# Memory keys and values of the prompt as plain float32 matmuls from unsplit weights, in four raw buffers

## The reference, cut to what matters

```python
def mem_kv(mem, lp):                      # mem: (1, 256, 1024)
    m = rmsnorm(mem, lp["mem_norm_g"])
    k = (m @ lp["w_mem_k"]).reshape(B, N_MEM, MEM_HEADS, MEM_HEAD_DIM)   # 1024 x 1024
    v = (m @ lp["w_mem_v"]).reshape(B, N_MEM, MEM_HEADS, MEM_HEAD_DIM)   # 1024 x 1024
    return k, v
```

## Time and profile before

| | us |
|---|---|
| median of 3 runs (lowest, highest) | 1037.19 (1035.57, 1038.5) |
| the profiled execution's own time | 1035.27 |
| its span, first to last instruction | 1033.5 |
| PE busy in the span | 993.0 (96%) |
| DVE, ACT, POOL busy | 514.6, 297.3, 442.5 |
| granted TensorE clock, mean | 0.994 of full |

### The profile page before, as it was taken

One profiled execution on the slowest core, in us unless ns is written; L12 is line 12 of the kernel. 1 busy time (PEld: TensorE's weight loads), 2 busy tenths in 40 slices (PEclk: granted clock), 3 DMA queues, 4 the chain that ended last, 5 costly groups with the idle time before them and its releaser, 6 DMA issues.

```text
span 1033.5 us, 19819 instructions
## 1 busy us (share of the span) xinstructions
PE 993.0 (96%) x8516; PEld 899.7 (87%) x8516; DVE 514.6 (50%) x724; ACT 297.3 (29%) x600; POOL 442.5 (43%) x282
## 2 busy tenths in 40 slices
PE   4999999889999999999999999999999999999997
PEld 4989998656777776999965799999999999999996
DVE  2889999467555555464156366431342134114413
ACT  5432375466444443121035222210120012002222
POOL 3445688500011112455420155655555555555551
PEclk9999999999899999999999999999999999999999
DMA  6422364422557772833193033223322332232222
GB/s 173 126 76 68 96 182 146 135 93 91 206 209 283 278 284 92 285 88 88 37 391 133 2 97 88 82 82 87 97 82 82 94 91 83 85 99 83 82 82 87
DMA packets 140556, 130.39 MB, mean 126 GB/s; under 512 B 13477, under 2 KB 133170, under 8 KB 136630
## 3 DMA queue, kind: packets, MB, share of 16 engines
q1 hardware_dynamic: 134888, 88.55, 28.5%
q0 software_dynamic: 2304, 37.75, 9.4%
q10 hardware_dynamic: 3278, 2.83, 0.8%
HBM read 123.53 MB, written 5.03 MB: 124 GB/s over the span
## 4 chain that ended last, share of the span: by engine, by line
PE 82%; DVE 10%; ACT 2%; issue 1%; POOL 1%; DMA 1%; SPq 1%; ACTq 1%; DVEq 0%; POOLq 0%
PE gps L558 56%; PE gps L893 5%; PE aux L907 3%; PE aux L934 3%; PE gps L1049 1%; PE aux L849 1%; PE gps L1131 1%; PE aux L913 1%; PE gps L871 1%; PE gps L969 1%; PE gps L682 1%; PE aux L1062 1%; PE aux L1083 1%; PE aux L924 1%; DVE lt L1718 1%
## 5 line engine op out<-in xcount | busy, mean ns | idle before, releaser
L487 POOL TENSOR_SCALAR whi<-wraw 128x1024 fp32r<-128x1024 f32 (+1 forms) x110 | 114.8, 1044 | 374.5 <-PE gps L558 303.3
L558 PE MATMUL gps<-act_hi,whi 128*128 128x272 f32 x912 | 265.4, 291 | 3.5 <-DVE act_lo L1636 2.8
L558 PE MATMUL gps<-act_lo,whi 128*128 128x272 f32 x912 | 264.4, 290 | 0.0
L558 PE MATMUL gps<-act_hi,wlo 128*128 128x272 f32 x912 | 263.8, 289 | 0.0
L490 POOL TENSOR_TENSOR wlo<-wraw,whi 128x1024 fp32r<-128x1024 f32 (+1 forms) x110 | 259.5, 2359 | 9.2
L558 PE MATMUL gps<-h_hi,whi 128*128 128x272 f32 x640 | 185.7, 290 | 0.0
L558 PE MATMUL gps<-h_lo,whi 128*128 128x272 f32 x640 | 185.1, 289 | 0.0
L558 PE MATMUL gps<-h_hi,wlo 128*128 128x272 f32 x640 | 184.6, 288 | 0.0
L558 PEld LDWEIGHTS gps<-act_hi,whi 128*128 128x128 f32 x912 | 172.4, 189 | 4.1 <-issue 3.1
L558 PEld LDWEIGHTS gps<-act_hi,wlo 128*128 128x128 f32 x912 | 172.4, 189 | 0.3 <-issue 0.2
L558 PEld LDWEIGHTS gps<-act_lo,whi 128*128 128x128 f32 x912 | 172.2, 189 | 0.0
(11 more groups left out here) (362 smaller groups left out, 1526.0 us busy)
## 6 DMA issues: line engine op xcount, KB each, us to landing
wraw<-in_w_up_dram SPq DMA_DIRECT2D x32, 512.0 KB, 4.0
wraw<-in_w_down_dram SPq DMA_DIRECT2D x32, 512.0 KB, 3.6
wraw<-in_w_in_dram SPq DMA_DIRECT2D x14, 512.0 KB, 4.0
kv<-in_cache_mem_k_dram SPq DMA_DIRECT2D x7, 1024.0 KB, 7.0
kv<-in_cache_mem_v_dram SPq DMA_DIRECT2D x7, 1024.0 KB, 13.2
wraw<-in_w_mem_k_dram SPq DMA_DIRECT2D x16, 256.0 KB, 3.0
wraw<-in_w_mem_v_dram SPq DMA_DIRECT2D x16, 256.0 KB, 3.1
wraw<-in_w_out_dram SPq DMA_DIRECT2D x8, 512.0 KB, 5.2
```

The costliest lines, as they stand in the source:

```text
L487: nc.gpsimd.tensor_scalar(whi[:, slot, 0:n], wraw[:, slot, 0:n], 1.0, 1.0, ALU.mult, ALU.mult).then_inc(pool_step, 1)
L558: mm = nc.tensor.matmul(out_of(a), w_of(w, k), x_of(x, k, part), start=(k == 0 and s == 0), stop=(k == k_tiles - 1 and s == 2))
```

## The change

The memory rows are written once, as float32 `mT`, without a `lo` part. The memory units are not split at all: each tile has 8 float32 matmuls where it had 24 `fp32r` ones. ACT's 32 roundings, POOL's 32 subtractions and DVE's 8 subtractions for `mT_lo` go away with the semaphores `w_half`, `w_hi`, `mem_half` and `raw_rest`. The room of `mT_lo` becomes `mraw`, two more raw buffers: memory unit `n` goes into `wraw` for `n % 4` of 0 and 1, and into `mraw` for 2 and 3. A unit is loaded by one transfer of 512 KB, and from the fifth on it waits until the tile four before is done. `ready(u)` is the count of `w_ready` once unit `u` is split, now that 16 units no longer count. PE waits for the transfer itself. The first two query units wait for the last memory tiles that read their `wraw` slots. In `gates`, the wait for `mn_lo` becomes one for `mn_ok`.

```diff
 def raw_count(u):
-    return 16 * sum(3 if U_QU <= v < U_UV else 1 for v in range(u % 2, u + 1, 2))
+    return 16 * sum(3 if U_QU <= v < U_UV else 0 if U_MK <= v < U_QU and (v - U_MK) % 4 > 1 else 1
+                    for v in range(u % 2, u + 1, 2))
+def ready(u):
+    return u + 1 - (16 if u >= U_QU else 0)
...
-        mT_hi = at("mT_hi", [128, KD, M], F32R, P0 + 20480)
-        mT_lo = at("mT_lo", [128, KD, M], F32R, P0 + 20480 + 8192)
+        mT = at("mT", [128, KD, M], F32, P0 + 20480)
+        mraw = at("mraw", [128, 2, 1024], F32, P0 + 20480 + 8192)
...
+        def raw_of(n):
+            return (wraw if n % 4 < 2 else mraw)[:, n % 2, :]
...
             def load_mem(n):
-                u = U_MK + n
-                for z in range(2):
-                    if n < 2:
-                        sp.wait_ge(w_ready, u - 1)
-                    else:
-                        sp.wait_ge((w_half, w_ready)[z], (n - 1, u - 1)[z])
...
+                if n < 2:
+                    sp.wait_ge(w_ready, ready(U_MK + n - 2))
+                elif n >= 4:
+                    sp.wait_ge(tile_done, T_MK + n - 3)
+                if n < 8:
+                    w = wmk_v[:, :, 128 * n:128 * n + 128]
+                else:
+                    k = 4 * (n % 2)
+                    w = wmv_v[:, k:k + 4, 128 * (n - n % 2 - 8):128 * (n - n % 2 - 6)]
+                sp.dma_start(raw_of(n).rearrange("p (k n) -> p k n", k=w.shape[1]), w
+                             ).then_inc((raw_in if n % 4 < 2 else mraw_in)[n % 2], 16)
...
             def load_heads(u, src):
-                sp.wait_ge(w_ready, u - 1)
+                if u < U_QU + 2:
+                    sp.wait_ge(tile_done, T_MK + 13 + u - U_QU)
+                else:
+                    sp.wait_ge(w_ready, ready(u - 2))
...
-            def split_rest(u):
...
                 if U_MK <= u < U_QU:
-                    split_rest(u)
                     continue
...
+            def raw_wait(n):
+                if n % 4 < 2:
+                    pe.wait_ge(raw_in[n % 2], raw_count(U_MK + n))
+                else:
+                    pe.wait_ge(mraw_in[n % 2], 16 * (n // 4 + 1))
             def mem_tile(n):
-                u, t = U_MK + n, T_MK + n
-                pe.wait_ge(w_half, n + 1)
+                t = T_MK + n
+                raw_wait(n)
                 free_tile(t)
-                out = gps[:, 2 * (t % 2), 0:M]
                 for k in range(KD):
-                    if k == KD // 2:
-                        pe.wait_ge(w_ready, u + 1)
-                    for s, (w, x) in enumerate(((0, 0), (1, 0), (0, 1))):
-                        mm = nc.tensor.matmul(out, weights(u % 2, 128, w, k, 0, 128), (mT_hi, mT_lo)[x][:, k, :],
-                                              start=(k == 0 and s == 0), stop=(k == KD - 1 and s == 2))
-                    if k == KD // 2 - 1:
-                        mm.then_inc(mem_half, 1)
+                    mm = nc.tensor.matmul(gps[:, 2 * (t % 2), 0:M], raw_of(n)[:, 128 * k:128 * k + 128], mT[:, k, :],
+                                          start=(k == 0), stop=(k == KD - 1))
                 mm.then_inc(tile_done, 1)
             def value_tile(n):
...
+                        mm = nc.tensor.matmul(gps[:, 2 * (p % 2) + m, 0:256], mT[:, k, 128 * m:128 * m + 128],
+                                              raw_of(n)[:, 256 * i:256 * i + 256], start=(k == 0), stop=(k == KD - 1))
                 mm.then_inc(tile_done, 1)
...
-                nc.scalar.activation(mT_hi[:, k, :], aux[:, k // 2, (k % 2) * 256:(k % 2) * 256 + 256], ACT.Copy,
-                                     scale=cols("mem_norm_g", k)).then_inc(mn_hi, 1)
-            def weight_hi(n, z):
...
+                nc.scalar.activation(mT[:, k, :], aux[:, k // 2, (k % 2) * 256:(k % 2) * 256 + 256], ACT.Copy,
+                                     scale=cols("mem_norm_g", k)).then_inc(mn_ok, 1)
...
-            for k in range(KD):
-                dve.wait_ge(mn_hi, KD)
-                V.scalar_tensor_tensor(out=mT_lo[:, k, :], in0=aux[:, k // 2, (k % 2) * 256:(k % 2) * 256 + 256],
-                                       scalar=cols("mem_norm_g", k), in1=mT_hi[:, k, :].bitcast(F32),
-                                       op0=ALU.mult, op1=ALU.subtract).then_inc(mn_lo, 1)
```

More of the change, by code:

```diff
@@ L254, in build @@
         raw_in = [sem(f"raw_in{i}") for i in range(2)]
-        raw_rest = [sem(f"raw_rest{i}") for i in range(2)]
-        w_ready, pool_step, w_half, w_hi = sem("w_ready"), sem("pool_step"), sem("w_half"), sem("w_hi")
+        mraw_in = [sem(f"mraw_in{i}") for i in range(2)]
+        w_ready, pool_step = sem("w_ready"), sem("pool_step")
         tile_done = sem("tile_done")
@@ L266, in build @@
             sem(f"nx_{s}") for s in ("hi", "lo", "sq", "acc", "ps", "var", "rt"))
-        mn_a, mn_d, mn_T, mn_hi, mn_lo = (sem(f"mn_{s}") for s in ("a", "d", "T", "hi", "lo"))
+        mn_a, mn_d, mn_T, mn_ok = (sem(f"mn_{s}") for s in ("a", "d", "T", "ok"))
         kr_swap, kr_ok = sem("kr_swap"), sem("kr_ok")
-        mem_half, mem_T, mem_ev, mem_out = sem("mem_half"), sem("mem_T"), sem("mem_ev"), [sem("mem_out0"), sem("mem_out1")]
+        mem_T, mem_ev, mem_out = sem("mem_T"), sem("mem_ev"), [sem("mem_out0"), sem("mem_out1")]
         xc_ok, lg_ps, lg_e, lg_r, lg_a, lg_v, lg_s, lg_u = (
@@ L694, in value_tile @@
                 for i in range(4):
-                    if i == 2:
-                        pe.wait_ge(w_ready, u + 1)
                     k = 4 * (n % 2) + i
                     for m in range(2):
[L699 to L705, removed]
+                        mm = nc.tensor.matmul(gps[:, 2 * (p % 2) + m, 0:256], mT[:, k, 128 * m:128 * m + 128],
+                                              raw_of(n)[:, 256 * i:256 * i + 256], start=(k == 0), stop=(k == KD - 1))
                 mm.then_inc(tile_done, 1)
@@ L772, in _ @@
                 t = T_UV + i
-                pe.wait_ge(w_ready, U_UV + 1)
+                pe.wait_ge(w_ready, ready(U_UV))
                 free_tile(t)
@@ L1142, in _ @@
                 else:
-                    pe.wait_ge(w_ready, u + 1)
+                    pe.wait_ge(w_ready, ready(u))
                     free_tile(t)
@@ L1265, in _ @@
             for k in range(KD):
-                nc.scalar.activation(mT_hi[:, k, :], aux[:, k // 2, (k % 2) * 256:(k % 2) * 256 + 256], ACT.Copy,
-                                     scale=cols("mem_norm_g", k)).then_inc(mn_hi, 1)
-            def weight_hi(n, z):
-                u = U_MK + n
-                if z == 0:
-                    act.wait_ge(raw_in[u % 2], 16 * (u // 2 + 1))
-                else:
-                    act.wait_ge(raw_rest[u % 2], 16 * (n // 2 + 1))
-                if z == 0 and n >= 2:
-                    act.wait_ge(mem_half, n - 1)
-                else:
-                    act.wait_ge(tile_done, last_tile(u - 2) + 1)
-                part = slice(512 * z, 512 * z + 512)
-                nc.scalar.copy(whi[:, u % 2, part], wraw[:, u % 2, part]).then_inc(w_hi, 1)
+                nc.scalar.activation(mT[:, k, :], aux[:, k // 2, (k % 2) * 256:(k % 2) * 256 + 256], ACT.Copy,
+                                     scale=cols("mem_norm_g", k)).then_inc(mn_ok, 1)
             def mem_copy(n):
@@ L1349, in _ @@
                 nc.scalar.activation(lrv[:, w, :], lrv[:, w, :], ACT.Sqrt, scale=0.25).then_inc(lg_s, 1)
-            for n in range(2):
-                weight_hi(n, 0)
-                weight_hi(n, 1)
             norm_root(0, rstd_qc[:, :])
```

30 lines of the change are left out of this document (9 added, 21 removed).

## The result

The changed kernel is slower. On the first chip it took 1044.0 us (median of 4 runs) where the kernel before took 1036.4: the ratio is 1.0068, with a 95% interval of 1.0054 to 1.0081. A second measurement on another chip (e9) gave 1041.8 against 1036.2, 1.0048 (1.0031 to 1.0064). The forecast was 1017 us with a range of 1013 to 1022; the time came near the rival called "float32 is dear", which had 1048 and a chance of 0.03.

What follows compares the result with a forecast made beforehand. PE's instruction list was taken as the bound (busy 96% of the span). Terms 17.2 + 2.8 - 0.7 + 0 + 0.7 = 20.0 us took the profiled 1035.3 to 1015.3, so 1017 us against the 1037.2 median, range 1013 to 1022.

Steps and rivals of the forecast that it cites:

- float32 is dear: Rival: memory-stage products run as four passes, 0.478 us each, losing 14.3 us and ending at 1048; chance 0.03.
- Part 1, the matmuls: Memory stage: 120 products at 0.215 us as float32 in place of 0.359 as three fp32r matmuls, 17.2 us gained.
- The dear bound of 0.2475 us: Dearest float32 matmul price seen, from a cross-attention block of eight; by it the matmul gain would be 13.3 us.
- The sentence on the Trainium skill: Its claim that true FP32 takes four passes, a loss of 14.3 us; set aside for the trace's price, kept as rival.
- the point of decision, 0.388: Price of a memory-stage product, in us, above which the change would turn slower than the kernel before.
- Part 2, the waits for the split: Memory stage: PE's 1.8 us of waits for wlo and 1.0 us of small gaps go, 2.8 us gained.
- Part 3, the transfers: Memory stage: unit loads and key-row stores nearly keep up with PE; -0.7 us, with 0 and -3 as bounds.
- the bound of 3 us: Largest loss allowed for memory-stage transfers, whose own term was -0.7 us.
- Part 4, DVE and ACT: Shorter memory stage: DVE speeds up once POOL is silent, and ACT keeps pace; term 0, bound a 1.5 us stall.
- the 0.8 us of slack: After the value tiles: query bank free by 162.4 us, PE asking for it at 163.2.
- Part 5, the third query tile: Query stage: its load leaves about 0.9 us sooner; 0 to 1.4 us to be had, 0.7 us taken as gain.

Runs made afterwards that it cites:

- e9: The changed kernel itself, measured once more on another chip; 1041.8 us against 1036.2 for the kernel before, 1.0048.
- e2: Changed kernel, but each memory-stage product again three fp32r matmuls, on stale rounded weights (output not the reference's); 1034.2 us against 1036.1 for the kernel before, 0.9973.
- e10: Changed kernel with ACT's four GELU roundings moved ahead of the last value copy; 1040.1 us, ratio 1.0031 to the kernel before.
- e11: As e10, but three fp32r matmuls of stale rounded weights for each float32 product; 1031.8 us against 1036.2 for the kernel before, 0.9943.
- e3: As e2, but one fp32r matmul for each product in place of three (output not the reference's); 1019.3 us against 1036.1 for the kernel before, 0.9849.
- e6: Changed kernel with POOL's 32 subtractions of the memory stage put back, their results unread; 1041.5 us in a single run.
- e4: Kernel before with only the last two value units unsplit, using a float32 copy of the memory rows made in one DVE addition; 1037.7 us against 1036.1, 1.0007.
- e5: Changed kernel with each of the 64 float32 products of the key tiles issued twice; 1068.3 us (2 runs).
- e12: e8 with ACT's first two tanh one unit later and the w_uk load ahead of the rope transfers; 1032.9 us against 1036.7 for the kernel before, 0.9967.
- e7: Kernel before with SP issuing the small tnat stores ahead of the rope transfers and the w_uk load; 1038.2 us against 1037.0, 1.0005.
- e8: e4 with its DVE addition in four parts, GELU roundings ahead of the last value copy, and tnat stores early; 1036.4 us against 1037.0 for the kernel before, 0.9994.

## Why the prediction was wrong

**Part 1, the matmuls: this step failed.** It took four records of the cross-attention for four products. They were two. The distance was right to 0.001 us, the price half of the true one, and the term of 17.2 us gained was a loss of 8.8 (8.7 between the profiles of the changed kernel and e2, 8.3 between the medians of e10 and e11). What a record is was never checked against the loops of the code. The dear bound of 0.2475 us did not help, since it rested on the same count. The sentence on the Trainium skill ("FP8 and Floating Point Precision", TensorE Precision Notes: true FP32 takes four passes) was waved off by the same misreading, "1.8 `fp32r` ones". With the count set right the trace is near it: 0.432 us are 3.6 times the 0.1196 of the earlier trace rows. A pass by itself is not seen in any trace here; two matmuls in the profile are. The rival "float32 is dear" had the right mechanism at 0.478 us, and named the point of decision, 0.388. With 0.432 in place of 0.478 its sum is 120 x 0.046 = 5.5 us lower, 1042.5, between the two medians of 1044.0 and 1041.8.

**Part 2, the waits for the split: right, and a little more than was put down.** They went. At the old price of the products the stage from tile 1 on is 46.1 us long in place of 49.3 (e2): 3.2 us for a term of 2.8.

**Part 3, the transfers: not decided by the changed kernel,** where PE is slow enough for any of it (DMA share 0.51). In e3, where PE is faster still than the forecast had it, the stage takes 2.6 us longer than forecast. That is inside the bound of 3 us, but most of the waits came from a limit that the forecast had not seen, two `knat` buffers for stores, and at the pace of the forecast nothing was measured.

**Part 4, DVE and ACT: the mechanism right, the margin wrong.** The operations of DVE fell to 0.22 us, and e6 shows that POOL was the reason. But the chain from the last value tile over ACT's roundings and `gl_lo` to the free query bank was put at 5.3 us and took 7.2 (182.41 to 189.57), and PE asked for the bank 0.6 us sooner after the value tiles than had been reckoned, so the 0.8 us of slack became a pause of 1.66 us. Partly this may be the lock once more: the four last subtractions took 3.76 us for 2.9, with POOL's split of the query units beside them.

**Part 5, the third query tile: the number right by luck.** It starts 7.2 us behind the tail transposes where it was 7.9, and 0.7 had been put down. But the way was another. The wait of 1.31 us for its split went wholly, and so did the one of 0.46 before the first query tile, which starts 0.4 us behind the tail transposes and not 1.05 as forecast. Against that stood the new wait of 1.66 us for ACT's bank. Without that wait, in e10, the third tile starts 5.4 us behind.

**What no part had** is the clock: about 3.4 us of the first profile's 8.6 us, behind two pauses of PE. At like clock the runs differ by about 5 us, so the price of the products explains the loss without it.

Does the change cause this? The pause at 188 us goes with e10, and the drop there with it. That makes the pause a condition of that drop; what makes a pause end in a drop is open. The length alone does not tell: behind a pause of 1.66 us the clock fell in the changed kernel, e9 and e6, and stayed full in e2, e4, e5 and e12. Behind 1.7 us it stayed full in the kernel before. Behind 1.96 us it fell in the changed kernel and stayed full in e5. Nor does the dense float32 stage ahead of the pause tell, since e5 has it as well. In the twelve runs of e9, time and clock go together (five at 0.992 took 1039.3 to 1041.8 us, five at 0.986 to 0.988 took 1043.5 to 1044.8). That the low clock, and not something else, makes the runs of one kernel spread over 5 us is argued from this and was not tried.

## What to carry to other kernels

Before a price is read from records, count them against the loop that issues them: a float32 matmul may be more than one record, and the count of the group shows it. At 128x128 by 256 columns, three `fp32r` matmuls on a hand-made split (0.359 us) beat one plain float32 product (0.432) on TensorE as long as other engines can make the halves in time. Plain float32 is worth a trial for the few tiles where PE waits for a split; in e12 that stage became 2.0 us shorter. An edit that frees one engine should be followed down the in-order lists of the others: here a gain first turned into a new wait in e4, e7 and e8, and in e7 and e8 it was a wait behind an instruction that stood ahead for no reason of its own.

## What the runs showed of the hardware

A float32 matmul of 128x128 by 256 columns is two matmuls in the profile, 0.216 us apart (0.432 us in all, against 0.1196 for an `fp32r` one); a float32 transpose of 128x128 is one. A pause of PE of 1.7 to 2.4 us in a dense stretch can be followed by a stretch at half clock that costs 1.7 us (the changed kernel, e9, e10), and need not be (e5, e12). With POOL subtracting beside it, a DVE operation on 128x32 took up to 1.1 us in place of 0.22 (e6). Beside a DVE addition of 128x2048 (3.4 us), six POOL subtractions took 10.3 us in place of 8.4 (e4). So the lock seems to work in both directions: in e4 it is POOL, and behind it PE, that waits for DVE.
